# Eight more modulation slots handled beside the first attention, eight fewer beside its output product

## The reference, cut to what matters

```
mod = (c @ w_ada + b_ada)[:, None, :]
sh_m, sc_m, g_m, sh_f, sc_f, g_f = jnp.split(mod, 6, axis=-1)
h = rms_norm_2(x) * (1 + sc_m) + sh_m
...
x = x + g_m * (y @ w_out)
h = rms_norm_2(x) * (1 + sc_f) + sh_f
...
x = x + g_f * ((jax.nn.silu(gate) * up) @ w_ffn_out)
```

## Time and profile before

| | us |
|---|---|
| median of 3 runs | 1828.05 (1827.4 to 1828.36) |
| the profiled execution, its own time | 1825.89 |
| its span, first to last instruction | 1824.1 |
| TensorE busy | 1751.8 (96% of the span) |
| VectorE busy | 956.1 (52%) |
| ScalarE busy | 723.8 (40%) |
| GpSimd busy | 688.3 (38%) |

### The profile page before, as it was taken

The page is one execution under the profiler, slowest core; times in us unless marked ns, Lnnn a source line. Parts: engine busy times, 40 slices in busy tenths (PEclk is TensorE's granted clock), DMA queues, the critical chain, the costliest instruction groups (busy, mean ns, idle before and its releaser), DMA issues. The chain is left out here.

```text
span 1824.1 us, 23408 instructions
## 1 busy us (share of the span) xinstructions
PE 1751.8 (96%) x8349; PEld 1416.4 (78%) x8349; DVE 956.1 (52%) x1746; ACT 723.8 (40%) x1244; POOL 688.3 (38%) x303
## 2 busy tenths in 40 slices
PE   7999999988999999999999999999999999999997
PEld 6777777777888766788888887888766788888886
DVE  5999688584679577633343322579665311101112
ACT  5433655523375553322222222466553333222221
POOL 3424111236430334555445554440212454444442
PEclk9999999999999999999999999999999999999998
DMA  6234010053332224455555542233211232232211
GB/s 246 81 104 139 24 32 28 24 196 128 104 104 93 81 81 140 136 194 189 194 187 185 187 148 81 87 110 104 93 35 35 69 108 100 81 115 93 93 58 47
DMA packets 56634, 197.67 MB, mean 108 GB/s; under 512 B 6993, under 2 KB 8017, under 8 KB 56530
## 3 DMA queue, kind: packets, MB, share of 16 engines
q1 hardware_dynamic: 55666, 194.15, 31.6%
q10 hardware_dynamic: 864, 2.11, 0.3%
HBM read 194.14 MB, written 2.10 MB: 108 GB/s over the span
## 5 line engine op out<-in xcount | busy, mean ns | idle before, releaser
L491 POOL TENSOR_TENSOR WL<-RAW,WH 128x1024 fp32r<-128x1024 f32 x234 | 592.5, 2537 | 900.6 <-ACT WH L580 561.8
L1743 PE MATMUL bank<-HH,WH 128*128 128x512 f32 x1120 | 437.0, 390 | 7.8 <-POOLq L496 5.9
L1745 PE MATMUL bank<-HH,WL 128*128 128x512 f32 x1120 | 435.9, 389 | 0.0
L1744 PE MATMUL bank<-HL,WH 128*128 128x512 f32 x1120 | 435.8, 389 | 0.0
L580 ACT ACTIVATE WH<-RAW 128x1024 fp32r<-128x1024 f32 x259 | 270.6, 1051 | 243.8 <-PE bank L1745 218.1
L1743 PEld LDWEIGHTS bank<-HH,WH 128*128 128x128 f32 x1120 | 210.2, 188 | 53.3 <-issue 10.2
L1745 PEld LDWEIGHTS bank<-HH,WL 128*128 128x128 f32 x1120 | 210.2, 188 | 44.0
L1744 PEld LDWEIGHTS bank<-HL,WH 128*128 128x128 f32 x1120 | 210.2, 188 | 43.4
L1676 DVE TENSOR_TENSOR HF<-SILU,bank 128x512 f32<-128x512 f32 x44 | 30.3, 688 | 314.3 <-PE bank L1745 311.3
L1743 PE MATMUL bank<-HDH,WH 128*128 128x512 f32 x352 | 137.1, 389 | 0.0
L1745 PE MATMUL bank<-HDH,WL 128*128 128x512 f32 x352 | 136.9, 389 | 0.0
(11 more groups left out here) (363 smaller groups left out, 2839.6 us busy)
## 6 DMA issues: line engine op xcount, KB each, us to landing
RAW<-in_stream SPq DMA_DIRECT2D x363, 512.0 KB, 3.3
out_t<-YA SPq DMA_DIRECT2D x8, 256.0 KB, 2.2
X<-in_xt ACTq DMA_DIRECT2D x3, 512.0 KB, 11.3
RAW<-in_stream SPq DMA_DIRECT2D x2, 256.0 KB, 4.0
X<-in_xt ACTq DMA_DIRECT2D x2, 256.0 KB, 6.4
ACC<-in_pos SPq DMA_DIRECT2D x1, 256.0 KB
gains<-in_gains SPq DMA_DIRECT2D x1, 224.0 KB
CS<-in_cs SPq DMA_DIRECT2D x1, 128.0 KB
```

The costliest lines, as they stand in the source:

```text
L491: nc.gpsimd.tensor_tensor(lo(k)[:], raw(k)[:], hi(k)[:].bitcast(F32), ALU.subtract).then_inc(sem["passed"], mark("passed", *k))
L1743: nc.tensor.matmul(out, A[0], B[0], start=first, stop=False)
L1744: nc.tensor.matmul(out, A[0], B[1], start=False, stop=False)
L1745: return nc.tensor.matmul(out, A[1], B[0], start=False, stop=last)
```

## The change

Block 1 (slots 8 to 15) of the first layer's modulation becomes a block that ScalarE and GpSimd handle beside the first attention. `ATT_ADA`, the list of the units at whose end a slot is scaled, goes from eight entries, every ninth unit (4, 13, 22, 31, 40, 49, 58, 67), to sixteen, every fifth (4, 9, 14, ... 79). In the stream sixteen slots instead of eight stand before o1,0, and behind the output tiles stand 2, 2, 2, 2, 0, 0, 0, 0 instead of 2, 3, 3, 3, 3, 2, 0, 0, the eight of block 2. By `mod_points` the block 0 accumulator is then turned at u = 43 (before: 71), block 1 at u = 83 (before: after o1,3) and block 2 after o1,4 (before: after o1,6). The first slot of block 1 waits for the same event as that of block 0, which lies before the attention.

```
-        order += [ada.pop(0) for _ in range((2, 3, 3, 3, 3, 2, 0, 0)[n])]
+        order += [ada.pop(0) for _ in range((2, 2, 2, 2, 0, 0, 0, 0)[n])]
...
-ATT_ADA = tuple(range(4, 76, 9))
+ATT_ADA = tuple(range(4, 84, 5))
...
-    return key[:2] == ("ada", 0) and key[2] // 8 in (0, MLA_CB)
+    return key[:2] == ("ada", 0) and key[2] // 8 in (0, 1, MLA_CB)
...
-                    if cb:
+                    if cb == MLA_CB:
                         act.wait_ge(sem["gated_in"], value("gated_in", 0, KD - 1))
                     else:
                         act.wait_ge(sem["head_sq_read"], value("head_sq_read", head_square(3, NT - 1)))
```

## The result

| | before | changed |
|---|---|---|
| median, us | 1828.2 (1824.7 to 1833.7, 20 runs) | 1832.4 (1831.1 to 1837.8, 20 runs) |
| ratio to before | | 1.0022, 95% interval 1.0012 to 1.0031 |
| profiled execution, its own time and span, us | 1825.89, 1824.1 | 1832.33, 1830.5 |

The change makes the kernel 0.22% slower. Against the prediction the median is 2.8 us above the forecast of 1829.6, inside the range, and just over the bound of 0.2%: "slower by over 0.2%" had 0.35, "same" 0.50. The sum itself missed by more. It gave +1.5 us where the medians differ by 4.2 and the two profiled executions by 6.4: the profiled execution came at 1832.33 where I had 1827.4. The range is 6.5 us wide, and part of the hit is luck, because the shift of 2.16 from the profiled execution to the median held for the kernel before alone; the changed kernel's profiled execution lies at its median.

The account below looks back on a forecast made before the run. Bound by a TensorE-VectorE chain in the attention to 300 us, later TensorE; in the output product TensorE with three gaps. Attention +6.1, output product -4.6, sum +1.5: execution 1827.4, median shifted by 2.16 to 1829.6 us, range 1826.5 to 1833.

Parts of the forecast that it names:

- The gain in the output product: Output product: two TensorE gaps and one accumulator turn go, together 4.6 us (bounds 3.5 and 6.6).
- The second and third gap: Output product: TensorE's waits of 1.08 and 2.50 us for weight splits both go, 3.58 us gained.
- the first gap: Output product: TensorE's wait of 1.94 us before o1,1, behind two modulation slots, stays.
- Adds that block VectorE: Attention: five more GpSimd adds at 0.68 us each block small VectorE operations; 4.0 taken, 3.4 us on the path.
- ScalarE's delay: Attention: six more scalings before unit 68 delay evictions for TensorE by 0.2 us each, +1.2 us (bounds 0 and 6.8).
- Scalings next to splits: Attention, units 74 to 75 and 79 to 80: TensorE waits about 1.0 and 0.4, +1.4 us (bounds 0 and 2.1).
- Block 0's turn leaving unit 71: Attention, unit 71: TensorE's waits for the last add, transposes and reductions go, -2.4 us.
- Block 0's turn at unit 43: Attention, unit 43: no wait, but two reductions and the bias in VectorE's row, +1.5 us.
- Block 1's turn at unit 83: Attention, unit 83: TensorE has no slack, +1.04 us; the reductions beside VectorE's idle time cost 0.
- what doesn't move: End of attention: GpSimd's splits and first MIX multiplication come some 8 us later, but the last multiplication depends on the last unit.
- The signs named beforehand: Profile after: only the 1.94 gap, unit 68 5 to 6 us later, blocked small operations, waits at units 76 and 81, none at turns.
- The clock, a rival with 0.05: Around the transposes of MIX: low-clock stretch falls otherwise against the work, 2 us either way; chance 0.05.

Follow-up runs that it names:

- no_adds: Changed kernel with GpSimd leaving out the seven adds of block 1, so its vector is incomplete; 1828.87 us, 1.0005 of before.
- fold_after: Changed kernel with line 1406 left out in branch 0, the gate folded into the operation that reads PSUM; 1825.27 us, 0.9979 of before.
- extra_matmuls: Changed kernel with 28 extra 128x512 bf16 matmuls, before the scores of every second unit up to 54; 1833.01 us, 1.0028 of before.
- fold_before: Kernel before with line 1406 left out in branch 0, the gate folded into the operation that reads PSUM; 1829.75 us, 1.0004 of before.
- placed: Changed kernel with gate folded, sixteen slots placed to avoid blocking adds, block 0's turn at unit 35, block 1's after o1,0; 1820.62 us, 0.9958 of before.
- turn_late: Changed kernel with block 1's accumulator turned after output tile o1,2 instead of at unit 83; 1832.68 us, 1.0013 of before.
- turns_both_late: Changed kernel with both turns in the output product, block 0's after o1,0 and block 1's after o1,2; 1834.88 us, 1.0035 of before.
- placed_before: Kernel before with gate folded, its eight slots at units 4 to 28 by fours and 31, block 0's turn at unit 35; 1825.88 us, 0.9994 of before.
- placed_turn43: Folded changed kernel with the sixteen placed slots, block 1's turn after o1,0, but block 0's turn at unit 43 instead of 35; 1823.98 us, 0.9968 of before.

## Why the prediction came out as it did, point by point

**The gain in the output product: right in kind, the size depends on the clock.** The second and third gap are gone, a turn is gone, and the first gap stayed. Forecast -4.6; measured 3.1 less in the profile of the changed kernel, where the clock was low for 3.4 us of this stage, and 5.1 to 5.3 less in no_adds, fold_after and extra_matmuls. The first gap is not fixed, as I had it: it is 2.39 here, since the transposes of MIX went faster and TensorE came to it earlier (5.15 us against 6.36, with 3.0 instead of 5.5 us of low clock):

```profile
381.47 5.15 PE L1829 MATMUL bank<-ident,MIX 128*128 128x128 f32 x32 [2.79 <-POOL MIX L552]
```

One reading was wrong without harm: the four operations of line 983 in 7.35 us are not 1.84 each, but three of 1.28 and one of 3.19 that stood behind GpSimd's split. The same lock works in this stage too, and in both directions.

**The attention: forecast +6.1, measured +9.3, of which 3 to 6 by the estimate above go with the clock.** By its terms:
- *Adds that block VectorE* was the right mechanism and the mis-sized term. I counted five more adds at 0.68 us and took 3.4; the blocked time grew by 4.8, because six of the eleven adds hit (four of six before) and a hit cost 1.5 us instead of 1.0. Passing on 85% of it by VectorE's share of busy time was no rule either. In units 8 to 31, where neither trace has low clock to speak of, two stalls of 2.4 us made the stretch 2.3 us longer than fold_after's; the stall of 1.75 us in units 48 to 55 cost 1.7, while the one at 316.89 made units 56 to 63 no longer at all. In units 32 to 39 a stall of 1.62 us stands beside a difference of 3.5, but there 6.7 us of low clock come with it, so that more than the stall itself is passed on is not shown. Whether VectorE's chain bounds the stretch decides, not its busy share; that reading fits the stages, and no run tested it by itself. The rule from the Trainium skill (SBUF — State Buffer, section "SBUF: two separate sides"), an exclusive lock held for the whole GpSimd operation, agrees with the seven rows: six of the blocked operations end within 0.04 us of GpSimd's, 2.13 us for line 997 among them, and the largest, line 1443 (0.42 us when free), 0.28 us behind it. Not every add hits, though: five of the eleven met nothing, and the price of 2.35 us for each did not come.
- *ScalarE's delay*, 1.2 forecast: 0.1 us between units 8 and 39 (56.3 us in fold_after, with seven scalings, against 56.1 in fold_before, with three). It shows next to the splits, and where scalings stand closer: placed, with one at every fourth unit and no stall or low clock in units 8 to 31, takes 40.1 us there against 39.1.
- *Scalings next to splits*, 1.4 forecast: TensorE waits 1.33 + 0.29 = 1.6 at the two places named. Right; moving the splits away gave 0.9 of it back.
- *Block 0's turn leaving unit 71*, -2.4 forecast: -3.7 (11.9 to 8.2); the slot of unit 67 left this stretch as well, so not all of it is the turn's.
- *Block 0's turn at unit 43*, +1.5 forecast: 0.3 by turn_late against turns_both_late. The 4 us and more of the placed kernels at unit 35 lie within what their low clock there can cost; what the turn adds to that stays open, since no two traces differ in it alone.
- *Block 1's turn at unit 83*, +1.04 forecast with its reductions hidden: units 80 to 87 grew by 2.6, and turn_late takes 2.0 of it away. The step that failed is "what doesn't move": I let GpSimd's split and its multiplications of MIX come 8 us later at no cost, and looked only at who waits for them. They came to lie on the turn's bias add and blocked it for 1.96 us, behind which TensorE waited 0.94.

**The signs named beforehand.** The gaps behind o1,1 went, five small operations lasted over 1 us, and TensorE waited at units 76 and 81, all as said. The maximum of unit 68 came 8.7 us later where I had 5 to 6, and TensorE waited at the turn of block 1 where I had none. The attention grew by 9.3 us, just under the 10 from which I would have called the prediction wrong. So the locks were the right mechanism; too small were the blocked time, the turn at unit 83 and the clock.

**The clock, a rival with 0.05, was given too little.** The mean granted clock of the runs is 0.9915 in the median for the kernel before (34 runs) and 0.989 for the changed one (20 runs). A straight line through the 34 runs of before gives 1.26 us per 0.001, with 0.8 us of scatter about it, so 0.0025 goes with 3.2 of the 4.2 us; at equal clock the two kernels would lie about 1 us apart. The profile that I read was one of the quickest executions of its kernel (1825.89, clock 0.994), with no low stretch in the attention before 370.5 us, in its last wait; the changed kernel's has three. So the stages of before are read from an execution quicker than most. Windows of the changed kernel at two of its three, in the columns of the earlier trace rows:

```profile
251.00:254.80 3.80, 3.80 (x21) 3.73 (x22) 3.19 (x10) 0.84 (x3) 0.00 (x0) 0.55 0.37 135
265.00:268.40 3.40, 3.40 (x12) 2.08 (x11) 1.09 (x3) 0.37 (x1) 0.00 (x0) 0.50 0.00 0
```

Whether this is a second cause beside the stalls or their consequence is open. For a consequence: the first stretch follows the stalls and waits of units 9 to 24, and the folded kernel, without them, has a mean clock of 0.9908 over its runs and no low stretch before 274 us. Against it: placed and placed_before have no blocked operation before unit 40 and low stretches from 251.6 and 248.4 us on, and placed_turn43, the same as placed until the turn at 258.51, has none before 267.3. No run varied the one without the other.

## What to carry to other kernels

An idle engine is not a free one: before moving work to GpSimd, lay each of its operations over VectorE's timeline and look for small operations that read SBUF alone (those on two SBUF inputs, and here one TENSOR_SCALAR on one), for these can stop until GpSimd's ends. Removing the operation that gets blocked (a factor folded into an operation that reads PSUM) can be worth nothing before a move and 7 us after it, so the two are to be tried together; here the move alone was 0.22% slower, with the fold 0.21% faster, with block 1's turn moved as well 0.37%, and with the slots placed too 0.42% (1821.79 and 1820.62 us; that last step is not resolved). A turn that must come in somewhere belongs into a wait of TensorE that exists already, after a check of what else waits for it; and stages of two executions are to be compared with their clock beside them.

## What the runs showed of the hardware that was not expected

The mean clock of a kernel whose TensorE is never idle for more than 2.8 us after the start of the attention moves from run to run between 0.988 and 0.995, and the time with it from 1834 to 1824 us, in unchanged code. Stretches at a granted 0.50, the level of 1.2 GHz, appear in the attention of the changed kernel behind waits of no more than 1.8 us between short matmuls. In three traces units 32 to 39 took 17.2, 21.2 and 24.0 us with 0, 6.7 and 13.7 us at 0.50 and no stall of VectorE in any of them. A TENSOR_SCALAR of 128x8 with one SBUF input stood 2.1 us behind a multiplication of GpSimd, and a split of GpSimd took 3.38 instead of 2.4 us beside an operation of VectorE. For a change of 0.2% one profile on each side says little, and a stage table of many is read with the clock of each.
